# A hybrid SSD, attention and MoE block: DVE's order in the attention, and the order of weight loads in the engines' loop

## The chip, the cores and the metric

The kernel runs on one core of a Trainium2 chip. The metric is the device time of one execution in microseconds (us); less is better. Input and output are float32 in DRAM.

## The reference

One layer on 512 tokens of width 1024: an SSD branch and a sliding-window attention branch side by side, merged, and behind them a mixture of 64 small experts with six experts for each token. Two parts of it matter here:

```python
# attention, in chunks of 64 queries against a band of 128 keys
scores = einsum("bckld,bcskd->...", qc, kb) * d ** -0.5 - slopes * dist
m = maximum(max(scores), sink)
pexp = exp(scores - m)
probs = pexp / (sum(pexp) + exp(sink - m))
out = einsum(probs, vb)
# experts
for e in range(64):
    hid = silu(n @ e_gate[e]) * (n @ e_up[e])
    out = out + (hid @ e_down[e]) * combine[:, e:e + 1]
```

## The kernel before

Every engine (PE, DVE, ACT, POOL and SP, which issues most DMAs) has an instruction stream of its own, written out by hand, and waits for the others by counting semaphores. What stands behind a wait on an engine waits too.

**The attention** goes over eight chunks of queries (`NCH`). For chunk c, PE does in this order: four of the eight steps of a product of the other branch (`ssd_branch`, L1702), the transposes of the chunk's softmax weights (`turn_weights`, L1680), the other four steps of `ssd_branch`, the product with the values (`values`, L1692) and the scores of chunk c+2 (`qk`, L1666). On DVE `scores(c)` adds the position bias to the scores in PSUM, reduces them to their maximum and ends with its negative (L1121 to L1127); ACT takes eight exponentials with their sums from that (`exponentials(c)`, L865), and `weights(c)` on DVE divides by the sum (L1132 to L1134), in the tile `prob`, a view of `seg` with one half for even and one for odd chunks. PE's transposes of chunk c wait for `prob_done`, the end of `weights(c)`. ACT's order for a chunk is: the exponentials of chunk c+1, the copy of chunk c's transposed weights out of PSUM (L877), for which `values(c)` waits by `pT_done`, and two more copies. Between chunks DVE also does two `late_step`s (L1143, L1146), each a multiply-add over a 512 KB load that POOL asks for, four ahead; 16 of the 32 stand behind the last chunk.

In DVE's loop `scores(c + 1)` stands ahead of `weights(c)`.

**The experts.** Rows of tokens are gathered for a unit of work, multiplied with gate and up weights (`gate_up`, L1862), and the hidden rows with the down weights (`down`, L1870). A unit is one expert with up to 128 rows or a pair of experts with up to 64 rows each; there are 42. The first 36 are written out (units 0 to 35). The last six are pairs, which all engines do in a loop (`Fori`) over a table of experts that is made from the routing; with these inputs the loop's body, six pairs, runs once. They are called pairs 36 to 41 here. PE's order in a unit n is: `gate_up(n)`, the transposes of the next unit's rows (L1850), `down(n-1)`, the transposes of unit n's hidden rows (L1877).

The weights lie in six slots, so three pairs' worth. One expert's gate, up and down weights are three loads of 1 MB each, all of them in SP's one queue. SP refills a slot's gate and up halves when PE's `gate_up` of its former user is done (semaphore `gu_ready`) and its down half when that unit's `down` is done (`ey_ready`). In the written-out part SP asks in iteration n for the gates and ups behind `gate_up(n)`, and then for the downs that go with the gates of iteration n-1, behind `down(n-1)`. In the loop it asked so:

```python
sp.wait_ge(gu_ready, j * LAST + (BEFORE - SLOTS // 2 + m + 1))
for i in range(2):
    load_gu(slots[i], ids[i])
sp.wait_ge(ey_ready, j * LAST + (BEFORE - SLOTS // 2 + m + 1))
for i in range(2):
    load_dn(slots[i], ids[i])
```

For m = 0 to 5 these are the weights of pairs 36+m; the first wait is for `gate_up(33+m)`, the second for `down(33+m)`, which PE does behind `gate_up(34+m)`.

**The end.** DVE scales each unit's rows (`rows_out`, L1360) and POOL scatters them to DRAM (L707), six rows for a token. When pair 39's scatter has landed, SP reads all rows back in twelve loads of 1 MB (`read_rows`, L527), again in its own queue; DVE and PE add them to the residual (L1438, L1465, L1969, L1974), DVE normalises, and the output is stored. The rows of pairs 40 and 41 are added from SBUF by PE.

Of the kernel before, what the change touches and what calls it, by code (L numbers as in the profile page):

```python
# [29 lines left out]
NCH = SEQ // CHUNK  # L30
# [22 lines left out]
SLOTS = 6  # L53
# [3 lines left out]
LAST = 6  # L57
SEQ0 = FIXED + 3 * PAIRED
KINDS = "FP" * FIXED + "SPSPSSP" * (PAIRED // 4)
BEFORE = len(KINDS)  # L60
# [29 lines left out]
def hybrid_ssd_swa_moe_adaln_block(nc, a):  # L90
# [51 lines left out]
    with ExitStack() as ctx:  # L142
# [3 lines left out]
        def sem(name):  # L146
            return ctx.enter_context(nc.semaphore(name))
# [77 lines left out]
        def flat(ap):  # L225
            return ap.rearrange("p a b -> p (a b)")
# [36 lines left out]
        def over(ap, n):  # L263

            return ap.unsqueeze(2).broadcast_to([ap.shape[0], ap.shape[1], n])
# [4 lines left out]
        def dn(s):  # L270
            return dn_lo[:, s - 2, :, :] if s in (2, 3) else dn_hi[:, s if s < 2 else s - 2, :, :]
# [97 lines left out]
        ht_ready, hT_done, ey_ready, ey_dve = sem("ht_ready"), sem("hidT_done"), sem("ey_ready"), sem("ey_dve")  # L369
# [38 lines left out]
        def _(sp):  # L408
# [54 lines left out]
            def which(src, e):  # L463
                return src[e] if isinstance(e, int) else src[bass.ds(e, 1)].rearrange("o p k f -> (o p) k f")

            def load_gu(s, e):
                sp.dma_start(gu(s)[:, 0, :, :], which(w_gate, e)).then_inc(gu_in[s], 16)  # L467
                sp.dma_start(gu(s)[:, 1, :, :], which(w_up, e)).then_inc(gu_in[s], 16)  # L468

            def load_dn(s, e):  # L470
                sp.dma_start(dn(s)[:, :, :], which(w_down, e)).then_inc(dn_in[s], 16)  # L471
# [8 lines left out]
            def expert(r):  # L480
                return sp.value_load(order[0:1, r:r + 1], min_val=0, max_val=NE - 1)  # L481

            ids = [expert(r) for r in FIRST]
# [8 lines left out]
            for un in range(BEFORE):  # L492
                ids = [expert(r) for r in REFILL[un]]
# [10 lines left out]
            with sp.Fori(0, count) as j:  # L504
                for m in range(LAST):
                    ids = [sp.value_load(table[0:1, bass.ds(j * (2 * LAST) + (2 * m + i), 1)], min_val=0,  # L506
                                         max_val=EMPTY) & (NE - 1) for i in range(2)]
                    slots = [SLOT[SEQ0 + 2 * m + i] for i in range(2)]
                    for i in range(2):
                        sp.to_reg(ids[i])  # L510
                    sp.wait_ge(gu_ready, j * LAST + (BEFORE - SLOTS // 2 + m + 1))
                    for i in range(2):
                        load_gu(slots[i], ids[i])
                    sp.wait_ge(ey_ready, j * LAST + (BEFORE - SLOTS // 2 + m + 1))
                    for i in range(2):
                        load_dn(slots[i], ids[i])
            units, each = count * LAST + BEFORE, count * (16 * LAST // 2) + 16 * BEFORE // 2
            others, free = each - 16, [units - 2, units - 1]
            sp.to_reg(units), sp.to_reg(others), sp.to_reg(free[0]), sp.to_reg(free[1])
# [448 lines left out]
        def _(dve):  # L968
            steps = [0]

            def chain(ins):

                steps[0] += 1
                ins.then_inc(dve_step, 1)
                dve.wait_ge(dve_step, steps[0])
# [138 lines left out]
            def scores(c):  # L1114
                s0 = CHUNK if c == 0 else 0
                dve.wait_ge(s_ready, c + 1)
                if c >= 2:
                    dve.wait_ge(pT_ready, c - 1)
                S = prob[:, c % 2, :, s0:]
                b = 2 + 2 * (c % 2)  # L1120
                dve.tensor_tensor(S, flat(ps[:, b:b + 2, :]).rearrange("p (j s) -> p j s", s=P)[:, :, s0:],  # L1121
                                  alibi[:, :, s0:], ALU.add).then_inc(s_read, 1)
                dve.wait_ge(s_read, c + 1)
                chain(dve.tensor_reduce(mx[:, c % 2, :], S, AX.X, ALU.max))
                chain(dve.tensor_tensor(mx[:, c % 2, :], mx[:, c % 2, :], sinkc[:, :], ALU.max))
                dve.tensor_tensor(dsink[:, c % 2, :], sinkc[:, :], mx[:, c % 2, :], ALU.subtract)
                dve.tensor_scalar(nmx[:, c % 2, :], mx[:, c % 2, :], -1.0, None, ALU.mult).then_inc(nmx_done, 1)  # L1127

            def weights(c):
                s0 = CHUNK if c == 0 else 0  # L1130
                dve.wait_ge(exp_done, c + 1)
                chain(dve.tensor_tensor(den[:, c % 2, :], rsum[:, c % 2, :], esink[:, c % 2, :], ALU.add))  # L1132
                chain(dve.reciprocal(den[:, c % 2, :], den[:, c % 2, :]))
                dve.tensor_tensor(prob[:, c % 2, :, s0:], prob[:, c % 2, :, s0:], over(den[:, c % 2, :], P - s0),  # L1134
                                  ALU.mult).then_inc(prob_done, 1)
# [3 lines left out]
            def late_step(m):  # L1139
                s, k = m // KC, m % KC  # L1140
                dve.wait_ge(late_in[m % 4], 16 * (m // 4 + 1))
                if k == 0:
                    dve.tensor_scalar(late_acc[:, s, :], h[:, m % 4, :], silc[:, 0:1], None, ALU.mult).then_inc(late_used, 1)  # L1143
                else:
                    dve.wait_ge(late_used, m)
                    dve.scalar_tensor_tensor(out=late_acc[:, s, :], in0=h[:, m % 4, :], scalar=silc[:, k:k + 1],  # L1146
                                             in1=late_acc[:, s, :], op0=ALU.mult, op1=ALU.add).then_inc(late_used, 1)

            scores(0)
            for c in range(NCH):  # L1150
                if c + 1 < NCH:
                    scores(c + 1)
                weights(c)
                for m in range(2 * c, 2 * c + 2):
                    late_step(m)
            for m in range(2 * NCH, NLATE):
# [861 lines left out]
```

## Time and profile before

| | us |
|---|---|
| median of 3 runs | 1268.61 |
| lowest and highest run | 1268.25, 1270.86 |
| the profiled execution, its own time | 1268.09 |
| its span in the trace | 1266.3 |
| PE busy | 1181.1 |
| DVE busy | 480.8 |
| ACT busy | 246.4 |
| POOL busy | 192.0 |

The span runs from the first to the last instruction of the trace; all times of rows count from its start. Idle time is given in square brackets ahead of an instruction, with what ended it; "issue" there is a wait of which the profile shows no releaser. "DMA share" is the busy share of the core's 16 DMA engines, over each of which every load is spread. A load's landing is counted when the last of them is done. A granted clock (PEclk) of 1.00 is 2.4 GHz, 0.50 is 1.2 GHz.

### The profile page before, as it was taken

The page shows a single profiled execution, that of the slowest core. Times are in us where ns is not written, and L with a number is a line of the kernel's source. Part 1 is how long each engine was busy: PE and PEld are TensorE (multiplying, and loading weights), DVE is VectorE, ACT ScalarE, POOL GpSimd, SP SyncE. Part 2 cuts the span into 40 slices and gives each one's busy share as a digit, 9 for nine tenths or more (in the row PEclk, how much of TensorE's full clock was granted, in tenths as well). Part 3 has the DMA queues.
Part 4 walks back from the last instruction along what each step waited for, and adds up shares of the span by engine and source line. Part 5 has one row for each costly group of instructions (what it writes and reads, how often), then busy time and mean ns, then how long its engine had stood idle before and what let it go on. Part 6 is the DMA issues. An engine that isn't in the chain of part 4 may idle for free. (4 is left out here: it accounts for less than half of the span.)

```text
span 1266.3 us, 13416 instructions
## 1 busy us (share of the span) xinstructions
PE 1181.1 (93%) x4799; PEld 606.4 (48%) x4799; DVE 480.8 (38%) x1007; ACT 246.4 (19%) x611; POOL 192.0 (15%) x320
## 2 busy tenths in 40 slices
PE   4999999998999999999999999999999998978896
PEld 2535875565554444458854434444444343423332
DVE  5677024565564411104765222322222222212257
ACT  2141122234340100001121221221212121201111
POOL 5000010201012000010261212122121112111100
PEclk9999999999999999999999999999999999988998
DMA  9732232214549932227256999999999999999966
GB/s 301 201 123 76 67 134 91 87 56 137 163 127 357 410 136 67 99 97 328 76 198 271 333 421 421 423 423 422 415 408 409 406 397 395 399 390 389 397 259 261
DMA packets 110985, 334.66 MB, mean 264 GB/s; under 512 B 14356, under 2 KB 67688, under 8 KB 83912
## 3 DMA queue, kind: packets, MB, share of 16 engines
q1 hardware_dynamic: 87824, 269.37, 55.4%
q0 software_dynamic: 18400, 47.10, 10.3%
q10 hardware_dynamic: 4696, 17.35, 3.4%
q8 instruction: 38, 0.62, 0.2%
q14 instruction: 27, 0.22, 0.0%
HBM read 314.49 MB, written 38.35 MB: 279 GB/s over the span
## 5 line engine op out<-in xcount | busy, mean ns | idle before, releaser
L1862 PE MATMUL ps<-gu_hi,xsT 128*64 128x512 f32 (+1 forms) x704 | 243.3, 614 | 26.1 <-DMA gu_hi<-in_exp_w_up_dram 10.3
L1862 PE MATMUL ps<-gu_lo,xsT 128*64 128x512 f32 (+1 forms) x320 | 149.0, 620 | 11.8 <-issue 6.3
L1862 PEld LDWEIGHTS ps<-gu_hi,xsT 128*64 128x64 f32 (+1 forms) x704 | 84.4, 155 | 134.9 <-issue 133.1
L1364 DVE SCALAR_TENSOR_TENSOR hid<-ps,wgt,gated 128x256 f32<-128x256 f32 x42 | 20.3, 484 | 306.1 <-ACT gated L942 306.1
L1870 PE MATMUL ps<-dn_hi,hidT 128*64 128x512 f32 (+1 forms) x352 | 119.9, 597 | 1.1 <-DVE hn L1360 1.1
L1509 PE MATMUL ps<-n1T,ring 128*128 128x512 f32 x256 | 111.9, 593 | 0.0
L1739 PE MATMUL ps<-n1T,ring 128*128 128x512 f32 x256 | 110.9, 592 | 0.7 <-ACT attT L882 0.7
L707 POOL DMA_INDIRECT expert_rows<-hn,meta x40 | 40.0, 1001 | 397.2 <-DVE hn L1360 352.0
L1360 DVE TENSOR_TENSOR hn<-ps,g_row 128x1024 f32<-128x1024 f32 x42 | 51.4, 1225 | 91.6 <-PE ps L1870 91.4
L1862 PEld LDWEIGHTS ps<-gu_lo,xsT 128*64 128x64 f32 (+1 forms) x320 | 51.7, 167 | 64.8 <-issue 64.7
L942 ACT ACTIVATE gated<-ps 128x256 f32<-128x256 f32 x42 | 16.1, 384 | 332.4 <-PE ps L1862 332.4
L1739 PEld LDWEIGHTS ps<-n1T,ring 128*128 128x128 f32 x256 | 48.6, 190 | 61.6 <-issue 60.7
L1509 PEld LDWEIGHTS ps<-n1T,ring 128*128 128x128 f32 x256 | 48.1, 190 | 58.7 <-issue 58.7
L1870 PE MATMUL ps<-dn_lo,hidT 128*64 128x512 f32 (+1 forms) x160 | 72.5, 596 | 0.2 <-DMA dn_hi<-in_exp_w_down_dram 0.2
L1517 PE MATMUL ps<-ring,n1T 128*128 128x256 f32 x320 | 70.3, 380 | 0.0
L932 ACT ACTIVATE xsT<-ps,mod 128x128 f32<-128x128 f32 x172 | 64.8, 457 | 28.5 <-PE ps L1850 28.5
L1517 PEld LDWEIGHTS ps<-ring,n1T 128*128 128x128 f32 x320 | 60.5, 190 | 9.2 <-issue 1.2
L1870 PEld LDWEIGHTS ps<-dn_hi,hidT 128*64 128x64 f32 (+1 forms) x352 | 38.7, 150 | 48.1 <-issue 46.2
L1354 DVE TENSOR_SCALAR xsT<-ps,mod 128x128 f32<-128x128 f32 x172 | 58.8, 404 | 7.2 <-PE ps L1850 7.2
L1702 PE MATMUL ps<-xbcT,ring 128*128 128x512 f32 x128 | 58.4, 599 | 0.0
L1754 PE MATMUL ps<-ring,raw 128*128 128x256 f32 x256 | 56.6, 380 | 1.7 <-DVE work L1196 1.7
L1850 PEld LDWEIGHTS ps<-ident,hn 128*128 128x128 f32 x344 | 42.9, 191 | 31.2 <-issue 27.5
(336 smaller groups left out, 1329.6 us busy)
## 6 DMA issues: line engine op xcount, KB each, us to landing
gu_hi<-in_exp_w_gate_dram SPq DMA_DIRECT2D x44, 1024.0 KB, 18.6
gu_hi<-in_exp_w_up_dram SPq DMA_DIRECT2D x44, 1024.0 KB, 30.8
dn_hi<-in_exp_w_down_dram SPq DMA_DIRECT2D x44, 1024.0 KB, 29.1
ring<-in_w_in_dram SPq DMA_DIRECT2D x21, 1024.0 KB, 5.5
gu_lo<-in_exp_w_gate_dram SPq DMA_DIRECT2D x20, 1024.0 KB
gu_lo<-in_exp_w_up_dram SPq DMA_DIRECT2D x20, 1024.0 KB
dn_lo<-in_exp_w_down_dram SPq DMA_DIRECT2D x20, 1024.0 KB
h<-in_ada_w_dram POOLq DMA_DIRECT2D x32, 512.0 KB, 5.4
```

The costliest lines, as they stand in the source:

```text
L707: pool.indirect_dma_start(out=rows_d[:, :], out_offset=bass.IndirectOffsetOnAxis(ap=meta[:, c, 1:2], axis=0), in_=ys[:, b, :], in_offset=N ...
L932: ins = act.activation(xsT[:, b, k, :], ps[:, 0, P * k:P * k + P], ACT.Identity, bias=B2[:, k:k + 1], scale=A2[:, k:k + 1])
L1354: ins = dve.tensor_scalar(xsT[:, b, k, :], ps[:, 1, P * (k - 4):P * (k - 4) + P], A2[:, k:k + 1], B2[:, k:k + 1], ALU.mult, ALU.add)
L1360: dve.tensor_tensor(ys[:, b, :], flat(ps[:, 5:7, :]), g2_row[:, :], ALU.mult).then_inc(ey_dve, 1)
L1509: ins = pe.matmul(bank, w[:, k, lo:lo + P], n1T[:, k, :], start=(k == 0), stop=(k == KC - 1))
L1517: ins = pe.matmul(bank[:, 0:WB], n1T[:, k, P * t:P * t + P], w[:, k, :], start=(k == 0), stop=(k == KC - 1))
L1702: ins = pe.matmul(ps[:, 1, :], w[:, k, P * (m % 2):P * (m % 2) + P], uT[:, k, :], start=(k == 0), stop=(k == KC - 1))
L1739: ins = pe.matmul(ps[:, 4 * jj + b, :], w[:, k, P * jj:P * jj + P], src[:, k, :], start=(k == 0), stop=(k == KC - 1))
L1754: ins = pe.matmul(ps[:, 2 * (t % 2) + b // 2, WB * (b % 2):WB * (b % 2) + WB], mergedT[:, k, P * t:P * t + P], w[:, k, :], start=(k == 0), ...
L1850: ins = pe.transpose(ps[:, k // 4, P * (k % 4):P * (k % 4) + P], xs[:, b, :].rearrange("p (f k) -> p k f", k=KC)[:, k, :], ident[:, :])
L1862: ins = pe.matmul(ps[rows, 2 + b, :], xsT[:, b, k, rows], gu(s)[:, :, k, :], start=(k == 0), stop=(k == KC - 1))
L1870: ins = pe.matmul(ps[rows, 5 + half, :], hidT[:, jj, rows], dn(s)[:, jj, BANK * half:BANK * half + BANK], start=(jj == 0), stop=(jj == 1))
```

## The change

Two places, both in the order of work; no instruction is added or taken away on DVE, and SP issues the same loads.

In the attention DVE does `scores(0)` and `scores(1)` first, and from then on `weights(c)` ahead of `scores(c + 1)`. In SP's loop the down weights of pair 36+m are asked for behind the gates and ups of pair 37+m; those of the last pair follow behind the loop's last pair. The semaphore values that the downs wait for are the same as before.

```diff
--- before.py
+++ after.py
@@ -511,9 +511,14 @@
                     sp.wait_ge(gu_ready, j * LAST + (BEFORE - SLOTS // 2 + m + 1))
                     for i in range(2):
                         load_gu(slots[i], ids[i])
-                    sp.wait_ge(ey_ready, j * LAST + (BEFORE - SLOTS // 2 + m + 1))
-                    for i in range(2):
-                        load_dn(slots[i], ids[i])
+                    if m >= 1:
+                        sp.wait_ge(ey_ready, j * LAST + (BEFORE - SLOTS // 2 + m))
+                        for i in range(2):
+                            load_dn(before[i][0], before[i][1])
+                    before = list(zip(slots, ids))
+                sp.wait_ge(ey_ready, j * LAST + (BEFORE - SLOTS // 2 + LAST))
+                for i in range(2):
+                    load_dn(before[i][0], before[i][1])
             units, each = count * LAST + BEFORE, count * (16 * LAST // 2) + 16 * BEFORE // 2
@@ -1147,10 +1152,11 @@
             scores(0)
+            scores(1)
             for c in range(NCH):
-                if c + 1 < NCH:
+                weights(c)
+                if 1 <= c < NCH - 1:
                     scores(c + 1)
-                weights(c)
                 for m in range(2 * c, 2 * c + 2):
                     late_step(m)
```

DVE, one chunk in the middle of the attention, before (L1121 to L1127 are `scores(c + 1)`, L1132 to L1134 `weights(c)`; lines of the changed kernel are higher by five):

```order
L1121 TENSOR_TENSOR seg<-ps,alibi 128x1024 [waits pT_ready,s_ready]
L1124 TENSOR_REDUCE mx<-seg 128x8 [waits s_read]
L1125 TENSOR_TENSOR mx<-mx,sinkc 128x8 [waits dve_step]
L1126 TENSOR_TENSOR dsink<-sinkc,mx 128x8 [waits dve_step]
L1127 TENSOR_SCALAR nmx<-mx 128x8
L1132 TENSOR_TENSOR den<-rsum,esink 128x8 [waits exp_done]
L1133 RECIPROCAL den<-den 128x8 [waits dve_step]
L1134 TENSOR_TENSOR seg<-seg,den 128x1024 [waits dve_step]
L1146 SCALAR_TENSOR_TENSOR siluz<-h,small,siluz 128x1024 [waits late_used,late_in2]
L1146 SCALAR_TENSOR_TENSOR siluz<-h,small,siluz 128x1024 [waits late_used,late_in3]
```

The same chunk in the changed kernel:

```order
L1137 TENSOR_TENSOR den<-rsum,esink 128x8 [waits exp_done]
L1138 RECIPROCAL den<-den 128x8 [waits dve_step]
L1139 TENSOR_TENSOR seg<-seg,den 128x1024 [waits dve_step]
L1126 TENSOR_TENSOR seg<-ps,alibi 128x1024 [waits pT_ready,s_ready]
L1129 TENSOR_REDUCE mx<-seg 128x8 [waits s_read]
L1130 TENSOR_TENSOR mx<-mx,sinkc 128x8 [waits dve_step]
L1131 TENSOR_TENSOR dsink<-sinkc,mx 128x8 [waits dve_step]
L1132 TENSOR_SCALAR nmx<-mx 128x8
L1151 SCALAR_TENSOR_TENSOR siluz<-h,small,siluz 128x1024 [waits late_used,late_in2]
L1151 SCALAR_TENSOR_TENSOR siluz<-h,small,siluz 128x1024 [waits late_used,late_in3]
```

The three instructions that make the weights have moved from behind the wait for `s_ready` (PE's `qk`) to ahead of it.

SP, the loads of the loop's last pair and what stands behind them (`dn_lo` and `dn_hi` are the slots' down halves):

```order
 L467 DMA gu_lo<-in_exp_w_gate_dram 128x2048
 L468 DMA gu_lo<-in_exp_w_up_dram 128x2048
+L471 DMA dn_lo<-in_exp_w_down_dram 128x2048 [waits ey_ready]
+L471 DMA dn_hi<-in_exp_w_down_dram 128x2048
 L471 DMA dn_hi<-in_exp_w_down_dram 128x2048 [waits ey_ready]
 L471 DMA dn_lo<-in_exp_w_down_dram 128x2048
```

Two pairs' downs stand now at the end, one behind the other; ahead of them each pair's gates and ups have moved up by one pair's downs.

## Rows read from the trace of the kernel before

**Rows 1.** the page: busy time of PE; two lines of its 40 equal slices

```profile
PE 1181.1 (93%) x4799; PEld 606.4 (48%) x4799; DVE 480.8 (38%) x1007; ACT 246.4 (19%) x611; POOL 192.0 (15%) x320
...
PEclk9999999999999999999999999999999999988998
DMA  9732232214549932227256999999999999999966
```

**Rows 2.** timeline of PE, DVE, ACT, one chunk: start, length, line, [idle, releaser]

```profile
320.74 3.70 PE L1702 MATMUL ps<-xbcT,ring 128*128 128x512 f32 x8
325.44 1.09 PE L1680 MATMUL ps<-ident,seg 128*128 128x128 f32 x8 [1.00 <-DVE seg L1134]
...
329.90 1.15 PE L1692 MATMUL ps<-turned,v_odd 128*64 128x64 f32 x32
...
320.85 1.23 DVE L1121 TENSOR_TENSOR seg<-ps,alibi 128x1024 f32<-128x1024 f32 x1 [5.03 <-PE ps L1666]
...
323.65 0.17 DVE L1127 TENSOR_SCALAR nmx<-mx 128x8 f32<-128x8 f32 x1
...
324.16 1.23 DVE L1134 TENSOR_TENSOR seg<-seg,den 128x1024 f32<-128x1024 f32 x1
325.30 2.67 DVE L1146 SCALAR_TENSOR_TENSOR siluz<-h,small,siluz 128x1024 f32<-128x1024 f32 x2
...
323.85 0.40 ACT L865 ACTIVATE seg<-seg,nmx 128x128 f32<-128x128 f32 x1 [4.30 <-DVE nmx L1127]
...
327.04 1.00 ACT L877 ACTIVATE turned<-ps 128x1024 f32<-128x1024 f32 x1
```

**Rows 3.** the line L1134 alone: who waited for it, us, times

```profile
  PE ps L1680: 6.8, 7
```

**Rows 4.** timeline of DVE and PE behind the attention

```profile
421.37 1.28 DVE L1146 SCALAR_TENSOR_TENSOR siluz<-h,small,siluz 128x1024 f32<-128x1024 f32 x1 [1.74 <-DMA h<-in_ada_w_dram]
...
430.61 1.88 PE L1724 MATMUL ps<-siluz,ones 128*128 128x512 f32 x4
```

**Rows 5.** timeline of PE in the engines' loop, pairs 36, 39, 40, 41

```profile
1130.58 9.35 PE L1862 MATMUL ps<-gu_hi,xsT 128*64 128x512 f32 x32 [8.81 <-DMA gu_hi<-in_exp_w_up_dram]
...
1179.45 7.09 PE L1862 MATMUL ps<-gu_hi,xsT 128*64 128x512 f32 x32 [0.98 <-DMA gu_hi<-in_exp_w_up_dram]
...
1195.57 0.61 PE L1862 MATMUL ps<-gu_lo,xsT 128*64 128x512 f32 x1 [3.92 <-DMA gu_hi<-in_exp_w_up_dram]
...
1205.37 3.65 PE L1870 MATMUL ps<-dn_hi,hidT 128*64 128x512 f32 x16
...
1210.97 0.61 PE L1862 MATMUL ps<-gu_hi,xsT 128*64 128x512 f32 x1 [1.52 <-DMA gu_lo<-in_exp_w_up_dram]
```

**Rows 6.** timeline of SP's DMA queue

```profile
1182.45 2.31 SPq L468 DMA_DIRECT2D gu_lo<-in_exp_w_up_dram  x1
...
1191.68 0.38 SPq L471 DMA_DIRECT2D dn_lo<-in_exp_w_down_dram  x1
...
1216.25 0.81 SPq L527 DMA_DIRECT2D gu_hi<-expert_rows  x2
```

**Rows 7.** windows: length, PE, PEld, DVE, ACT, POOL busy, PEclk, DMA share, GB/s

```profile
1188.00:1200.00 12.00, 8.08 (x32) 2.96 (x30) 2.48 (x7) 1.56 (x5) 2.36 (x4) 0.86 1.01 423
...
1206.00:1208.00 2.00, 2.00 (x13) 0.58 (x9) 0.84 (x3) 0.98 (x3) 0.00 (x0) 1.00 0.27 115
1216.00:1216.50 0.50, 0.50 (x4) 0.17 (x2) 0.00 (x0) 0.00 (x0) 0.00 (x0) 1.00 0.00 0
1217.00:1217.50 0.50, 0.50 (x6) 0.17 (x2) 0.00 (x0) 0.00 (x0) 0.00 (x0) 1.00 1.13 213
```

**Rows 8.** timeline of POOL, the scatter of pair 39's rows

```profile
1211.84 0.99 POOL L707 DMA_INDIRECT expert_rows<-hn,meta  x1 [15.15 <-issue]
```

**Rows 9.** the chain that ended last, and DVE's timeline there

```profile
1223.14 22.43 DMA gu_hi<-expert_rows
...
1245.59 5.04 DVE L1438 TENSOR_TENSOR h<-h,gu_hi 128x1024 f32<-128x1024 f32 x4 [1.08 <-DMA gu_hi<-expert_rows]
```

## The prediction

> **What bounds the kernel now.** I read the page first. PE is busy for 1181.1 us of a span of 1266.3, and the DMA engines are full for its last third [rows 1]. So time can be won where PE waits, or, late in the kernel, where the DMA engines do. The timeline of the attention comes next, since one half of the change is there. PE's stream is one piece but for one gap a chunk: it ends its four steps of `ssd_branch` at 324.44, and its transposes start at 325.44, after 1.00 us of waiting for L1134, the end of `weights` [rows 2]. The line's own view puts 6.8 us on seven such waits [rows 3]. Then the engines' loop: PE starts pair 36 at 1130.58 and pair 41 at 1210.97, both as their last gate or up load lands [rows 5]. Five pairs take 80.4 us, 16.1 each, while PE's own work on a pair is 1195.57 less the wait of 3.92 and less 1179.45, so 12.2, of which 7.09 are the gates and ups and 3.65 the downs [rows 5]. There the loads set the pace. Last the end of the loop, by the windows of the DMA engines and the chain: the read-back of the rows, and behind it DVE's adds [rows 6 to 9].
>
> **Part 1, the attention.** Before, `weights(c)` stands behind `scores(c + 1)`, which waits for PE's `qk`, so it can't start before PE is at `ssd_branch(c)`: scores 320.85 to 323.82, weights until 325.39, and PE needs them at 324.44 [rows 2]. What `weights` needs itself is the chunk's exponentials. Those of chunk c+1 are done at 327.04, where ACT goes on to its copy [rows 2], 6.3 us behind the start of `ssd_branch(c)`. In the new order DVE has its two late steps behind the scores: 323.82 + 2.67 = 326.5. So the next weights run from 327.1 to 327.1 + 1.66 = 328.8 (1.66 is 325.39 less 323.73), and PE wants them not before about 335.6, when the next four steps are over. The wait goes, with some 6 us of cover.
>
> What could be late next is ACT's copy of the transposed weights, which stands behind the exponentials of the next chunk. The scores still start as `qk` ends, since the weights are out of the way by then, so the copy still ends at 328.04. PE needs it 1.00 earlier than before, at 328.90 [rows 2]. 0.86 us are left, and no new wait comes. How many chunks: seven waits of 6.8 us, six of them of 1.00 (chunks 1 to 6), which is 6.0, and 0.8 for chunk 0, whose order of `scores(1)` and `weights(0)` stays. Chunk 7 has no scores ahead of its weights. **Gain 6.0 us.** It is PE's time, and what follows hangs on PE. The late steps end at 421.37 + 1.28 = 422.65 and are wanted at 430.61 [rows 4]: if they did not move up at all, PE would want them at 424.6 and still find them. The bounds of this part are 0 (ACT's copy or another thing takes the gap) and 6.8 (all of it goes).
>
> **Part 2, the loads.** Every load is spread over 16 DMA engines. Until 1200 all are busy (share 1.01), but at 1206 to 1208 the share is 0.27, while PE still waits until 1210.6 for pair 41's last load, asked for at 1182.45 [rows 5, 6, 7]. So a few engines lag some 10 us behind the others, and a load has landed when these are done with it. They set the loop's pace. The time of 1 MB on them is at most 16.1/6 = 2.7 us.
>
> Ahead of the gates and ups of pair 37+m now stand 2 MB less, the downs of pair 36+m. So those of pairs 37 to 41 land 2 x 2.7 = 5.4 us earlier on the lagging engines; they are asked for early enough, since SP no longer waits for a `down` ahead of them, and they are in the queue for about 28 us (1182.45 to 1210.6). The downs come 2 MB behind the next pair's gates, 5.4 us, and PE needs them about 8.1 us after these (12.2 less 3.65 and an estimated 0.4 for the short transposes behind). They are not waited for. So PE does pair 41 about 5.4 us earlier, at 1205.6 in before's times.
>
> But the end is set by what comes behind. After pair 41's gates and ups, the last downs are owed: 2 MB before, so until about 1216 on the lagging engines, and the windows agree: the share is 0.00 at 1216.0 to 1216.5 and 1.13 at 1217.0 to 1217.5, when the read-back starts [rows 7], issued at 1216.25 [rows 6]. The sum of all bytes ahead of the read-back is unchanged. So however early PE is, the lagging engines start it at 1215.5 to 1216 and not at 1217. The issue itself waits for pair 39's scatter: started 1211.84 [rows 8], behind `down(39)`, which runs 1205.37 to 1209.0 [rows 5]; 5.4 us earlier gives 1206.4, and the issue about 1211. That is early enough. The lagging engines gain their idle time of 1.0 to 1.5 us, and something of the ramp behind it. I take 2.0. DVE has at present a wait of 1.08 for the tenth load of the read-back (landing at 1223.14 + 22.43 = 1245.57) and has no other wait that matters from there to the last normalisation [rows 9]. DVE and PE would be there 5 us earlier, so that landing sets the end, and it comes 2.0 earlier. **Gain 2.0 us**; bounds 0 and 5.4. I am near the lower end since the rows of the windows show how little idle time there is to be had.
>
> By the Trainium skill ("DMA: Bandwidth & Descriptors", section "Queues, rings and completion order") each of the 16 engines consumes its own ring of a queue in order. By that rule a reorder within the queue moves landings but not the time at which the lagging engines are through, which is the 2.0; without it, by PE's gain alone, the part would be 5.4. The windows agree with the rule where 0.27 of the engines are busy and a landing is still out.
>
> **The sum** is made against the profiled execution: 1268.09 - 6.0 - 2.0 = 1260.1. It is 0.5 below the median of the runs, so the median to expect is 1260.6, and I say 1260.5.
>
> **The rivals.**
>
> A. *The attention alone gains*: 1262.6. In the new order PE's waits for loads are spread otherwise: none before pair 37, about 1 us before 38, about 4 us before 39 and 40 and 3 before 41. Before, a wait of 8.81 was followed by gates and ups of 9.35 instead of 7.09 us, at a clock of 1.2 GHz for a while [rows 5]. If that follows each of three waits, pairs 39 to 41 are later by 2 to 3 us each, partly absorbed by the waits themselves, and the scatter of pair 39 comes late enough to start the read-back at 1216 again. For it: the windows give a clock of 0.86 behind a wait of only 3.92 [rows 5, 7]. Against it: the margin is 5 us. Chance 0.2. The Trainium skill ("TensorE: Matmul & The Clock Gate", "HAM oscillation") states that waits for loads which recur can bring the clock down each time; that is the rule that speaks against this half, and here it would cost what is said above.
>
> B. *The loads gain in full*: 1268.6 - 6.0 - 5.4 = 1257.2. The lagging engines are not the same ones all the time, or the read-back, started at 1211 on the others, relieves them. For it: ten loads of the read-back take 28.6 us (1217.0 to 1245.57), 2.9 each, against 2.5 at the 423 GB/s of a full window [rows 7, 9], so there is something to relieve. Against it: the 0.00 window. Chance 0.15.
>
> C. *The attention's gap moves to another wait*: PE waits for ACT's copy before `values` instead of for the weights. It decides if the scores start more than 0.86 late. If DVE's weights were still in the way (1.66 late), PE would wait 0.8, six times: 4.8 of the 6.0 are lost, 1265.4. Chance 0.08.
>
> D. *Slower than before*: the downs, now behind the next pair's gates and ups, are what PE waits for. It decides when 2 MB need more than 8.1 us on the lagging engines instead of 5.4. Slower by more than 8 + 2.6 us in sum takes over 2.1 us on each of five pairs, 10.2 us for 2 MB. With 11 us the time would be 1268.6 - 6.0 + 5 x 2.9 = 1277.1. Rows 5 speak against it: no interval of pairs shows such a pace. Chance 0.02.
>
> E. *It does not do what it says*: the lagging engines' idle time and PE's gap return elsewhere, and the time stays at 1268.6. Chance 0.03.
>
> **How the numbers follow.** The forecast has 0.52, A 0.2, B 0.15, C 0.08, E 0.03, D 0.02. The range takes in A (1262.6) and B (1257.2) with half a microsecond to a whole one for the runs, 1256.6 to 1263.6. About 0.2% or 2.5 us is what a measurement of this kernel can tell from no change. A, B, C and the forecast are faster by more: 0.95 of the chance, of which I take 0.02 for shapes of C in which less is left. Faster 0.93, same 0.05, slower 0.02.
>
> **What the changed profile would show.** Right: L1680 (now another line number) has no wait for DVE in chunks 1 to 6, chunks come every 11.1 us instead of 12.1, ACT's copy ends ahead of PE's `values`. Pair 41's gates start some 11 us earlier in absolute time than 1210.97 (6.0 and 5.4), the read-back's DMA starts some 8 earlier than 1217.0, with no window at 0.00 between, and DVE waits 3 to 5 us for read-back loads instead of 1.08. Wrong: a wait of PE before L1692, or for down weights at L1870; a read-back that starts 6 us earlier only (A) or 11 us earlier on all engines (B).

## The result, and the profile after

The change takes 1257.9 us (median of 4 runs, 1256.99 to 1258.93), the kernel before beside it 1269.36 (4 runs, 1268.25 to 1270.86): the ratio is 0.9915, interval 0.9903 to 0.9927. A second measurement of the change gave 1257.67 and 0.9912 (0.9896 to 0.9929). I said 1260.5, with a range of 1256.6 to 1263.6: the sign and the range hold, and the time is some 2.6 us below the forecast.

The profiled execution took 1258.93 us, the slowest of the four; its span is 1257.2; PE is busy for as long as before [rows 1], and the DMA engines are full for the same third. From the page of the changed kernel:

```profile
PE 1181.8 (94%) x4799; PEld 607.9 (48%) x4799; DVE 481.3 (38%) x1007; ACT 246.1 (20%) x611; POOL 191.6 (15%) x320
...
DMA  9732242224559942237256999999999999999966
```

**The attention.** The timeline of the changed kernel, the same chunk as in [rows 2] (PE, DVE, ACT; start, length, line, then idle time and its releaser in brackets where there was one):

```profile
320.40 3.70 PE L1708 MATMUL ps<-xbcT,ring 128*128 128x512 f32 x8
...
323.94 1.04 PE L1686 MATMUL ps<-ident,seg 128*128 128x128 f32 x8
...
324.81 3.60 PE L1708 MATMUL ps<-xbcT,ring 128*128 128x512 f32 x8
...
328.34 1.15 PE L1698 MATMUL ps<-turned,v_odd 128*64 128x64 f32 x32
...
320.52 1.23 DVE L1126 TENSOR_TENSOR seg<-ps,alibi 128x1024 f32<-128x1024 f32 x1 [2.92 <-PE ps L1672]
...
323.39 2.67 DVE L1151 SCALAR_TENSOR_TENSOR siluz<-h,small,siluz 128x1024 f32<-128x1024 f32 x2
326.83 0.17 DVE L1137 TENSOR_TENSOR den<-rsum,esink 128x8 f32<-128x8 f32 x1 [0.78 <-ACT esink L872]
...
327.27 1.22 DVE L1139 TENSOR_TENSOR seg<-seg,den 128x1024 f32<-128x1024 f32 x1
...
323.51 0.40 ACT L870 ACTIVATE seg<-seg,nmx 128x128 f32<-128x128 f32 x1 [4.29 <-DVE nmx L1132]
...
326.71 1.00 ACT L882 ACTIVATE turned<-ps 128x1024 f32<-128x1024 f32 x1
```

PE goes from `ssd_branch` (L1708) to the transposes (L1686) with no wait. The weights (L1137 to L1139) run from 326.83 to 328.49, right behind ACT's exponentials; the prediction said 327.1 to 328.8. ACT's copy ends at 327.71 and PE's `values` (L1698) start at 328.34, 0.63 us later. A chunk takes 328.34 less 317.42, 10.92 us, where it took 329.90 less 317.76, 12.14, before. The line that makes the weights, alone (who waited for it: us, times), answers to [rows 3]; what is left is chunk 0:

```profile
  PE ps L1686: 0.8, 1
```

**The engines' loop.** PE's timeline at the gates of pairs 36, 38, 39, 40 and 41 (pair 37 starts at 1138.40 without a wait), which answers to [rows 5]:

```profile
1123.70 9.66 PE L1868 MATMUL ps<-gu_hi,xsT 128*64 128x512 f32 x32 [8.23 <-DMA gu_hi<-in_exp_w_up_dram]
...
1150.99 0.61 PE L1868 MATMUL ps<-gu_hi,xsT 128*64 128x512 f32 x1 [0.40 <-DMA gu_lo<-in_exp_w_up_dram]
...
1167.12 1.94 PE L1868 MATMUL ps<-gu_hi,xsT 128*64 128x512 f32 x3 [3.93 <-DMA gu_hi<-in_exp_w_up_dram]
...
1183.20 0.77 PE L1868 MATMUL ps<-gu_lo,xsT 128*64 128x512 f32 x1 [2.54 <-DMA gu_hi<-in_exp_w_up_dram]
...
1198.67 0.61 PE L1868 MATMUL ps<-gu_hi,xsT 128*64 128x512 f32 x1 [1.58 <-DMA gu_lo<-in_exp_w_up_dram]
```

There is no wait for down weights. To compare the loops I count from the start of the merge behind the attention, 389.31 before and 382.87 after, so that the attention's gain is left out. So counted, pair 41 starts at 821.7 before and 815.8 after, 5.9 us earlier (5.4 were forecast). Windows of the changed kernel (length; busy time of PE, PEld, DVE, ACT, POOL; PEclk, DMA share, GB/s): the gates and ups of pairs 38, 39 and 40, then the end of the drain and the start of the read-back, which answers to [rows 7]:

```profile
1150.99:1158.08 7.09, 7.09 (x33) 2.69 (x33) 0.73 (x3) 0.02 (x1) 2.36 (x4) 1.00 1.01 423
1167.12:1175.56 8.44, 8.44 (x33) 2.87 (x33) 0.00 (x0) 0.00 (x0) 1.00 (x1) 0.84 1.01 410
1183.20:1191.98 8.78, 8.78 (x33) 3.17 (x33) 0.00 (x0) 0.00 (x0) 1.61 (x4) 0.81 0.85 353
...
1204.00:1206.00 2.00, 2.00 (x12) 0.68 (x8) 0.00 (x0) 0.21 (x1) 0.00 (x0) 1.00 0.13 53
1206.00:1208.00 2.00, 2.00 (x14) 1.13 (x14) 1.60 (x5) 1.30 (x5) 0.00 (x0) 1.00 0.07 29
1207.50:1208.00 0.50, 0.50 (x4) 0.14 (x2) 0.50 (x3) 0.50 (x3) 0.00 (x0) 1.00 0.04 16
1208.00:1208.50 0.50, 0.50 (x4) 0.14 (x2) 0.25 (x1) 0.38 (x2) 0.00 (x0) 1.00 1.53 229
```

Pair 38, behind a wait of 0.40, has the full clock and its 7.09 us; pairs 39 and 40, behind waits of 3.93 and 2.54, have 0.84 and 0.81 and take 8.44 and 8.78. The engines' share falls below 0.15 at 1204, and of 16 engines 0.07 is one: the last one or two are still busy when the read-back begins.

**The read-back.** Of the changed kernel, POOL's timeline (the scatter of pair 39), SP's queue, the chain that ended last (start, length, what), and DVE's timeline, which answer to [rows 8, 6, 9]:

```profile
1199.47 0.99 POOL L712 DMA_INDIRECT expert_rows<-hn,meta  x1 [13.78 <-issue]
...
1180.69 1.55 SPq L471 DMA_DIRECT2D dn_lo<-in_exp_w_down_dram  x1
1207.27 0.81 SPq L532 DMA_DIRECT2D gu_hi<-expert_rows  x2
...
1199.47 7.75 DMA expert_rows<-hn,meta
1207.24 0.03 issue
1207.27 0.34 SPq L532
...
1212.43 23.98 DMA gu_hi<-expert_rows
...
1220.22 5.00 DVE L1444 TENSOR_TENSOR h<-h,gu_hi 128x1024 f32<-128x1024 f32 x4 [0.69 <-DMA gu_hi<-expert_rows]
...
1229.04 5.00 DVE L1444 TENSOR_TENSOR h<-h,gu_lo 128x1024 f32<-128x1024 f32 x4 [2.57 <-DMA gu_lo<-expert_rows]
...
1236.43 5.05 DVE L1444 TENSOR_TENSOR h<-h,gu_hi 128x1024 f32<-128x1024 f32 x4 [1.07 <-DMA gu_hi<-expert_rows]
```

Before, the scatter started at 1211.84 [rows 8] and the read-back was issued at 1216.25 [rows 6], 4.4 us later. Now the scatter starts at 1199.47, and 7.75 us pass until it lands and releases the issue. Counted from the merge, the scatter starts 5.9 earlier, the issue 2.5 earlier (824.4, before 826.9), and DVE's wait for the tenth load ends 2.7 earlier (853.6, before 856.3). So the scatter's earlier start of 5.9, less the 3.4 by which its landing took longer (7.8 instead of 4.4), is the 2.5. DVE waits 0.69, 2.57 and 1.07 us for loads, 4.3 in all (3 to 5 forecast).

### The profile page after: what moved, and what is told of

The parts are those of the page before. It is cut to its first block and busy times, and to the rows that moved or that the text cites. A ratio compares the mean times of both kernels' runs of the same rounds, so it can differ in the third digit from the quotient of the medians.

```text
span 1257.2 us, 13416 instructions
## 1 busy us (share of the span) xinstructions
PE 1181.8 (94%) x4799; PEld 607.9 (48%) x4799; DVE 481.3 (38%) x1007; ACT 246.1 (20%) x611; POOL 191.6 (15%) x320
## 2 busy tenths in 40 slices
DMA packets 110985, 334.66 MB, mean 266 GB/s; under 512 B 14356, under 2 KB 67688, under 8 KB 83912
## 5 line engine op out<-in xcount | busy, mean ns | idle before, releaser
L947 ACT ACTIVATE gated<-ps 128x256 f32<-128x256 f32 x42 | 16.1, 383 | 327.1 <-PE ps L1868 327.1
L1708 PE MATMUL ps<-xbcT,ring 128*128 128x512 f32 x128 | 58.4, 599 | 0.0
```

Source lines behind the costliest of these rows:

```text
L1708: ins = pe.matmul(ps[:, 1, :], w[:, k, P * (m % 2):P * (m % 2) + P], uT[:, k, :], start=(k == 0), stop=(k == KC - 1))
```

## The experiments

Nine kernels, each timed beside the kernel before. First the two halves of the change, each alone.

### The attention alone

Kernel before, with the change's order in DVE only:

```diff
             scores(0)
+            scores(1)
             for c in range(NCH):
-                if c + 1 < NCH:
+                weights(c)
+                if 1 <= c < NCH - 1:
                     scores(c + 1)
-                weights(c)
```

Expected:

> The kernel before with the new order of the attention alone; the loop asks for its downs as before. In the profile of the change the attention is 7.3 us shorter than before (first scores to the merge: 87.9 against 95.3), not 6.0. If nothing behind it gives that back, this kernel is 7.3 us faster than before. Rival: the stages behind are bound by transfers that do not move up, and the gain is 6 us or less. Second rival: the attention is worth more than its PE time, 9 us or more, since it also moves the loads.

Measured: 1261.44 us (5 runs, 1260.63 to 1262.4), before 1268.75; ratio 0.9943 (0.9929 to 0.9956), so 7.3 us less. From the first scores to the merge the attention took 389.31 less 294.05, 95.3 us, before, and 382.87 less 294.94, 87.9, in the changed kernel: 7.3 too. This half is worth 7.3 us and not the 6.0 of my sum. Behind the merge (383.24) the end comes as it did: the read-back is issued at 1209.77, 826.5 from the merge, before 826.9.

### The loads alone

Kernel before, with the downs one pair later in SP's loop, DVE as before. The edit is the first piece of the change's diff.

> The kernel before with the new order of loads in the loop alone. Theory of the lagging DMA engines: PE starts pair 41's gates 5 to 6 us earlier than before (1210.97), the read-back 2 to 3 us earlier than 1217.0, and the time falls by 2 to 3 us. Rival (all of PE's lead counts): 5.4 us or more. Rival (all is lost at the read-back): within 1 us of before.

Measured: 1265.3 us (10 runs, 1263.87 to 1267.01), ratio 0.9971 (0.9962 to 0.9981): 3.5 us less, interval 2.4 to 4.8. The halves add up: 7.3 and 3.5 are 10.8, and the whole change has 0.9912 to 0.9915 of 1268.75, 10.8 to 11.2. Its scatter starts at 1207.29 and its read-back is issued at 1214.78, 7.5 us later, as in the changed kernel; from the merge (390.46) the issue is at 824.3. This was not the full 5.4 of rival B, and half a microsecond more than the 2 to 3 expected.

### The changed kernel again

The changed kernel, word for word, as a second measurement beside the runs that leave work out below.

> The changed kernel itself once more, so that it stands beside the others of this call and has more runs: 10 to 11.5 us under before, the sum of its two halves measured alone (7.3 and 3.5).

Measured: 1257.67 us (4 runs, 1255.56 to 1259.0). The issue of the read-back is at 1207.22, the waits at the gates 8.59, 3.94, 2.20 and 1.55 us. From the merge (383.31) the scatter starts at 816.4 and the issue comes at 823.9.

### Scores 1.2 us later

What is next in the attention, and how near? In the changed kernel one more addition over 1024 columns stands between the wait for `qk` and the scores, in chunks 2 to 7:

```diff
                     dve.wait_ge(pT_ready, c - 1)
+                    dve.tensor_tensor(work[:, 4 * SEQ:4 * SEQ + D], flat(alibi[:, :, :]), flat(alibi[:, :, :]), ALU.add)
```

> The change with one more add of 1024 columns on DVE (1.2 us, its result unused) between the wait for a chunk's scores and the scores themselves, in chunks 2 to 7. In the changed kernel ACT's copy of the turned weights ends 0.63 us ahead of PE's values. If ACT's copy is next in line, PE waits about 0.6 us a chunk before the values, 3.6 us in all against the change. If there is more cover than that (the copy is not what comes next), the time stays within 1 us of the change.

Measured: 1261.11 us (5 runs), ratio 0.9938 (0.9924 to 0.9952), 3.2 to 3.4 above the two measurements of the change. PE's waits in the attention, by the waits view of that kernel (waiter <- releaser: us in total, times, longest), and its timeline in one chunk:

```profile
PE ps L1699 <- ACT turned L882: 2.9, 6, 0.5
...
328.86 1.00 ACT L882 ACTIVATE turned<-ps 128x1024 f32<-128x1024 f32 x1
...
329.92 0.50 PE L1699 MATMUL ps<-turned,v_odd 128*64 128x64 f32 x9 [0.49 <-ACT turned L882]
```

So the copy (L882) is what comes next, as rival C had it. Some 1.2 us of delay met a slack of 0.63 and left 0.6; the rows show 0.49 for each of six chunks, 2.9 in all, and 3.2 to 3.4 were measured, which the intervals of the ratios do not tell apart.

This kernel's loop is word for word the change's, and its profiled execution differs there mainly in one thing: PE did the gates and ups of pair 40 at the full clock. From its windows, its queues of POOL and SP, and its windows around the issue of the read-back:

```profile
1186.87:1193.96 7.09, 7.09 (x33) 2.68 (x33) 0.00 (x0) 0.00 (x0) 1.95 (x4) 1.00 0.93 387
...
1201.44 0.99 POOL L712 DMA_INDIRECT expert_rows<-hn,meta  x1 [11.74 <-issue]
...
1209.10 0.81 SPq L532 DMA_DIRECT2D gu_hi<-expert_rows  x2
...
1209.00:1209.50 0.50, 0.50 (x6) 0.20 (x4) 0.00 (x0) 0.00 (x0) 0.00 (x0) 1.00 0.12 49
```

Counted from the merge (386.67), pair 40 starts at 800.2, in the change at 800.3. It takes 7.09 us instead of 8.78, the scatter starts at 814.8 instead of 816.6, and the read-back is issued at 822.4 instead of 824.4, while two of the 16 engines (0.12) are still busy. So what released the issue was not the end of the lagging engines' work: it came with the landing of pair 39's scatter, whose start hangs on PE, 7.7 us behind that start. In the change these are 7.8 us, in its repetition 7.5 and in the loads alone 7.5.

### Downs two pairs later

Does the wait of rival D exist, and from which point? In the changed kernel the downs of a pair are asked for behind the gates and ups of the pair after the next:

```diff
-                    if m >= 1:
-                        sp.wait_ge(ey_ready, j * LAST + (BEFORE - SLOTS // 2 + m))
-                        for i in range(2):
-                            load_dn(before[i][0], before[i][1])
-                    before = list(zip(slots, ids))
+                    if m >= 2:
+                        sp.wait_ge(ey_ready, j * LAST + (BEFORE - SLOTS // 2 + m - 1))
+                        for s, e in waiting.pop(0):
+                            load_dn(s, e)
+                    waiting.append(list(zip(slots, ids)))
```

(and two such groups behind the loop).

> The change with the loop's downs asked for two pairs later instead of one. By the queue in order, a pair's downs then land about 16 us behind the next pair's gates and PE, which wants them 8.1 us behind these, waits for them at every pair from 36 on. The loads still set the pace, but the down of pair 39 and its scatter come some 8 us later than in the change, so the read-back starts 2 to 4 us later and the time is 2 to 4 us over the change. Rival (order in the queue does not matter, since the DMA engines are full anyway): the same time as the change, and no wait of PE for downs.

Measured: 1261.12 us (5 runs), ratio 0.9935 (0.9922 to 0.9949), 3.2 to 3.4 above the change. PE's timeline of that kernel at its waits in the loop:

```profile
1152.09 5.49 PE L1878 MATMUL ps<-dn_hi,hidT 128*64 128x512 f32 x16 [5.12 <-DMA dn_hi<-in_exp_w_down_dram]
...
1167.71 0.61 PE L1878 MATMUL ps<-dn_lo,hidT 128*64 128x512 f32 x1 [1.59 <-DMA dn_hi<-in_exp_w_down_dram]
...
1184.26 1.08 PE L1878 MATMUL ps<-dn_hi,hidT 128*64 128x512 f32 x1 [4.35 <-DMA dn_lo<-in_exp_w_down_dram]
...
1200.28 3.65 PE L1878 MATMUL ps<-dn_hi,hidT 128*64 128x512 f32 x16 [1.01 <-DMA dn_hi<-in_exp_w_down_dram]
```

Now PE waits at the downs (L1878), 12.1 us in all, and no longer at the gates of pairs 38 to 41. The mechanism of rival D is real and begins one pair further on. Its price is small against 12.1, since a wait at the downs takes the place of one at the next gates, but it is all that the loads' half had gained: the scatter of pair 39 stands behind such downs, and the read-back is issued at 826.9 from the merge (383.80), where it was before.

### Without the scatters

What makes a few DMA engines lag? This is the changed kernel with the scatters' bound at row 0, so that the units' output rows are not written to DRAM (that part of the computation is left out; the instructions and their descriptors stay):

```diff
-            last_token, last_row = pool.to_reg(SEQ - 1), pool.to_reg(NROW - 1)
+            last_token, first_row = pool.to_reg(SEQ - 1), pool.to_reg(0)
...
-                    in_=ys[:, b, :], in_offset=None, bounds_check=last_row, oob_is_err=False).then_inc(scattered[b], 16)
+                    in_=ys[:, b, :], in_offset=None, bounds_check=first_row, oob_is_err=False).then_inc(scattered[b], 16)
```

> The change with all scatters of the experts' rows bounded to row 0, so that next to nothing is written (left out: the rows of units 0 to 39 in DRAM, which stay zero); the scatter instructions, their waits and semaphores stay. Theory 1: the engines that lag do so because of the scatters, which fall unevenly on the 16. Then the share falls from 1 to 0 within 2 or 3 us at the end of the expert loads instead of some 17, the gates of pair 41 start 8 us earlier or more against those of the change, and the time falls by about as much. Theory 2: the lag comes from elsewhere (gathers, or engines slow by themselves): the ramp of the share stays over 10 us long, and the time falls by 1 to 4 us, for the bytes that are not written.

Measured: 1219.1 us (4 runs, 1217.5 to 1219.42), ratio 0.9614 (0.9598 to 0.9631), 38.6 below the changed kernel beside it. The windows of that kernel at the end of its loads (columns as above), and PE's timeline at the gates of pair 41:

```profile
1158.00:1160.00 2.00, 1.33 (x7) 0.60 (x9) 0.00 (x0) 0.00 (x0) 1.32 (x3) 1.00 0.99 418
1160.00:1162.00 2.00, 2.00 (x12) 0.84 (x10) 0.00 (x0) 0.00 (x0) 1.04 (x1) 1.00 0.87 361
1162.00:1164.00 2.00, 2.00 (x12) 0.85 (x10) 0.00 (x0) 0.00 (x0) 0.00 (x0) 1.00 0.47 177
1164.00:1166.00 2.00, 2.00 (x11) 0.68 (x8) 0.00 (x0) 0.21 (x1) 0.00 (x0) 1.00 0.27 111
...
1158.66 0.61 PE L1868 MATMUL ps<-gu_hi,xsT 128*64 128x512 f32 x1 [2.68 <-DMA gu_lo<-in_exp_w_up_dram]
```

Pair 41's last load lands some 0.3 us ahead of its gates, at 1158.3, while all engines are still busy; in the changed kernel it landed at 1198.3, some 9 us after the share had begun to fall. So most of the unequal load of the engines comes with the scatters, as I supposed, but not all is shown to: the share falls from full to 0.27 in some 5 us and stands there when the read-back is issued at 1165.47, so that the rest of the drain can't be seen. The bytes cost more than the lag: 12.4 MB less are moved (322.29 instead of 334.66 by the pages), which is 29 us at the 423 GB/s of a full window [rows 7], and that makes three quarters of the 38.6. I had expected a gain of 8 us or more, about as much as the lag, and had left the bytes out. The remaining 9 us go by the name of lag here without a run that shows it.

### Without the last pair's downs

Is it the backlog on the lagging engines that starts the read-back? In the changed kernel the downs behind the loop, 2 MB, are left out, and pair 41 uses the weights of pair 38 that lie in these slots:

```diff
-                sp.wait_ge(ey_ready, j * LAST + (BEFORE - SLOTS // 2 + LAST))
-                for i in range(2):
-                    load_dn(before[i][0], before[i][1])
```

> The change without the loads of the last pair's down weights, 2 MB (left out: pair 41 is computed with the downs of pair 38, which lie in its slots). If the read-back is held up by the lagging engines' backlog, that ends 4.9 us earlier here, the scatter of pair 39 lands 3 to 4 us after its start instead of 7.8, the read-back starts 4 to 5 us earlier than in the change, and the time falls by 4 to 5 us. If PE's chain to the scatter is what holds it and the scatter takes 7.8 us anyway, the read-back starts at the same time and the gain is under 1 us.

Measured: 1254.57 us (4 runs), ratio 0.9893 (0.9876 to 0.991), 3.1 below the changed kernel beside it. Its scatter starts at 1198.76. From its timeline, the issue of the read-back on SP's queue, and DVE's adds behind it:

```profile
1204.90 0.81 SPq L529 DMA_DIRECT2D gu_hi<-expert_rows  x2
...
1219.71 7.51 DVE L1441 TENSOR_TENSOR h<-h,gu_hi 128x1024 f32<-128x1024 f32 x6
...
1234.62 5.00 DVE L1441 TENSOR_TENSOR h<-h,gu_hi 128x1024 f32<-128x1024 f32 x4
```

DVE has no wait for a load left. Counted from the merge (384.01) the issue is at 820.9 instead of 824.4, but not all of these 3.5 us belong to the loads: here too pair 40 had the full clock, and the scatter started at 814.8 instead of 816.6. The execution of "Scores 1.2 us later" has that start and all loads; against it the scatter landed in 6.1 instead of 7.7 us, and the issue came 1.5 earlier. So bytes behind which a scatter stands do lengthen its landing, by some 1.5 us for these 2 MB, but neither expectation came out: it was to land in 3 to 4 us by the first and in 7.8 by the second. From there on DVE's adds are the bound, one behind the other, so that shorter waits for the read-back's loads alone would give nothing more.

### Neighbouring entries 8 partitions apart

Can the lag be cured? A unit's filled rows lie at the low partitions of each half of 64, and I supposed that neighbouring partitions go by the same DMA engine. In the changed kernel the upper and the lower three bits of an entry's place in its 64 change sides:

```diff
+                dve.tensor_scalar(up, at, 3, 0xE00, ALU.logical_shift_left, ALU.bitwise_and)
+                dve.tensor_scalar(down, at, 3, 0x1C0, ALU.logical_shift_right, ALU.bitwise_and)
+                chain(dve.tensor_scalar(at, at, 0x1F03F, None, ALU.bitwise_and))
+                chain(dve.tensor_tensor(up, up, down, ALU.bitwise_or))
+                dve.tensor_tensor(at, at, up, ALU.bitwise_or).then_inc(ordered, 1)
```

(`at` is the place of the entry, 64 to a block, by 64, plus the expert.)

> The changed kernel, with the place of an entry in its list of 64 rewritten as it is chosen: of the six bits of the place the upper three and the lower three change sides, so that neighbouring entries come to stand 8 partitions apart instead of side by side (five small DVE instructions more per tile of tokens, two of them on the path before the lists are read, together under 1 us). The gathers and scatters of a unit still move as many rows, but these are spread over all partitions. Theory 1 (the engines lag because a unit's filled rows lie in the low partitions of either half, and so on the same DMA engines unit after unit, while all sixteen share the weights evenly): the fall of the DMA share ahead of the read-back, which took from about 1190 to 1207 us, shrinks to a few us; the area under it (share 0.3 to 0.5 over some 17 us) is 8 to 10 us that all engines together do not need, so pair 41 is gated 3 to 8 us earlier and the read-back's loads are issued 4 to 9 us earlier, until DVE and PE bound the end: 1249 to 1254 us. Rival (the engines lag for another reason, such as packets of a scatter that take long on any engine): the ramp stays as it is and the time is that of the changed kernel or up to 1 us above it, 1257.5 to 1258.7 us.

Measured: 1270.02 us (11 runs, 1269.18 to 1271.64), ratio 1.0015 (1.0006 to 1.0024): 12 to 13 us above the change, all of its gain gone. The loop begins 0.9 us later; the rest is lost while loads stream, as the windows of this kernel and of the changed one show (40 us each, the second pair of rows is the changed kernel's):

```profile
1060.00:1100.00 40.00, 36.99 (x133) 15.88 (x132) 8.40 (x21) 6.44 (x17) 6.39 (x12) 0.91 0.96 367
1100.00:1140.00 40.00, 30.03 (x108) 12.69 (x108) 8.03 (x19) 4.94 (x13) 7.67 (x13) 0.87 0.98 379
```

```profile
1060.00:1100.00 40.00, 37.13 (x146) 17.26 (x145) 10.25 (x25) 7.19 (x19) 7.09 (x12) 1.00 1.00 397
1100.00:1140.00 40.00, 31.77 (x127) 12.41 (x127) 9.47 (x24) 6.42 (x17) 5.31 (x9) 0.87 1.00 400
```

Packets and bytes are the same (110985, 334.66 MB), but 367 and 379 GB/s are moved where the change has 397 and 400, and the share has fallen to 0.96 and 0.98. Engines without work account for about half of the lower rate (4 and 2% of 8 and 5%); for the other half they were busy and moved less, which no run explains. Its drain is no shorter and comes later; the read-back is issued at 1219.69. So where the filled rows lie does matter, and this placement makes it worse, where I had assumed the opposite.

### Places mixed by expert

From that I formed another theory, that row p goes by engine p modulo 16, and had the lower four bits of a place mixed with the expert's number:

```diff
+                dve.tensor_scalar(low, low, 6, 0x3C0, ALU.logical_shift_left, ALU.bitwise_and)
...
+                dve.tensor_tensor(at, at, low, ALU.bitwise_xor).then_inc(ordered, 1)
```

> The changed kernel, with the lower four bits of an entry's place in its list combined (exclusive or) with the lower four bits of its expert's number, by two small DVE instructions more per tile of tokens. The same rows are moved from the same half; which residues of the partition by 16 the filled ones take now differs by expert. With neighbouring entries 8 partitions apart the time was 12 us above the change at the same packets and bytes, so placement matters, but not as assumed. Theory 1 (row p of a gather or scatter goes by DMA engine p modulo 16): by the counts of this input's lists the most loaded engine had 217 of the 3072 rows, mean 192; with entries 8 apart 307, here 196. At 4 KB a row in each direction and 423 GB/s over 16 engines (26.4 GB/s each) an excess of 25 rows is 7.8 us of one engine, of 115 rows 36 us, of 4 rows 1.2 us. The most loaded engine sets when a unit's weights are complete, so up to 6.6 us of lag go: the drain ahead of the read-back is 3 to 6 us shorter, the time 1252 to 1255.5 us. Rival (8 neighbouring partitions by one engine, as assumed before): mixing the lower four bits keeps each group of 16 on two engines, nothing changes: 1257 to 1258.5 us. Second rival (the order of addresses in DRAM matters, since neighbouring entries of a list no longer follow each other): no gain, or a loss.

Measured: 1258.12 us (5 runs, 1257.5 to 1259.08), ratio 0.992 (0.9906 to 0.9933): the same as the change. Its share falls from 0.94 at 1188 to 1190 to 0.17 at 1204 to 1206, nearly the ramp of the change. This theory falls too: it wanted 3 to 6 us. With neither assumed map can both runs be explained. Others, such as one by blocks of four neighbouring partitions, were not tried, nor was the second rival, the order of addresses in DRAM, told apart from them; which engine serves which row stays open. No version here beats the change.

## Why the prediction was right, and where it was off

- **Part 1, the attention: the mechanism was right, its size 1.3 us too small** (6.0 in the sum, 7.3 by the run of this half alone). The step that failed is "six of them of 1.00, which is 6.0". A bracketed wait of PE counts from the modelled end of the matmuls ahead of it, 320.74 + 3.70 = 324.44 [rows 2]. Where PE doesn't wait, the next group starts before that end: in the change at 323.94, when the group ahead ends at 324.10, and it is 1.04 long instead of 1.09. 1.00 + 0.16 + 0.05 is 1.21 a chunk, the 1.22 that the two periods show. Six of them are 7.3. The kernel before shows it too, at chunk 7, where PE has no wait: the transposes start at 383.06, when the group ahead (379.52 + 3.70) ends at 383.22. My bound of 6.8, all the waits of the line's own view, was no bound for that reason.
- The cover was right. Weights ran at the forecast times, the copy's slack was 0.63 (forecast 0.86), and a delay of 1.2 us brought out exactly this wait, six times. So rival C was the next thing in line, but did not happen.
- **Part 2, the loads: right in sign, too small, and for a reason that did not hold** (2.0 in the sum; 3.5 by the run of this half, 2.4 to 4.8; 2.7 between the profiled executions). PE came 5.9 us earlier to pair 41 (5.4 forecast) and gained only half of it at the end, as forecast. The step that failed is "So however early PE is, the lagging engines start it at 1215.5 to 1216 and not at 1217". The read-back was issued at 824.4 from the merge, which in before's times is 1213.7, and its DMA followed at about 1214.4; and it was the scatter of pair 39, which hangs on PE's `down(39)`, that released it, not the end of the lagging engines' work, as the execution with pair 40 at the full clock shows (scatter 1.8 earlier, issue 2.0 earlier, two engines still busy).
- The other half of the same step is "5.4 us earlier gives 1206.4, and the issue about 1211. That is early enough": it took the 4.4 us from the scatter's start to the issue as they were before, but a scatter that starts while engines are busy takes longer to land. The starts at 822.5 to 823.4 from the merge (before, the attention alone, downs two pairs later) have the issue 3.1 to 4.4 us behind them, at 826.5 to 826.9; the five at 814.3 to 816.8 (the change, its repetition, the loads alone, scores later, places by expert) have it 7.5 to 7.8 us behind. So 5.9 less 3.4 is what the order gave in the profiled executions. That 2.0 was near 2.5 is luck: the term was the idle time of the lagging engines, and it was not this that was gained. Why the runs give 3.5 and the profiled executions 2.7 isn't shown; the change's profiled execution is the slowest of its four, with a mean clock of 0.983 against 0.985 to 0.987.
- The time of 1 MB on the lagging engines, "at most 16.1/6 = 2.7 us", held as the value for landings. Pair 41 was 5.9 us earlier from the merge, but pair 36, which the order can't touch, was 0.4 earlier as well (741.3 and 740.8); the rest is 5.4, in the loads alone 5.5 and in the repetition 5.6, for the 5.4 forecast. It isn't the time by which 2 MB less shorten the end (1.5 in the run without the last downs).
- The rule of the Trainium skill ("DMA: Bandwidth & Descriptors", "Queues, rings and completion order"), that each engine consumes its ring of a queue in order, gave the 2.0, against 5.4 without it. The landings agree with it: 5.4 to 5.6 us earlier for 2 MB less in front, and with the downs two pairs later it was these that PE waited for. The 3.5 measured lies between the two. The rule is about one queue; the scatters come by another, and my use of it left them out.
- **Rival A** (1262.6) named something that happened: the clock of pairs 39 and 40 fell to 0.84 and 0.81 behind waits of 3.93 and 2.54, at a cost of 1.4 and 1.7 us each. Pair 39's cost went into the next wait for loads. Pair 40's did not: it delayed the scatter of pair 39, and where the clock held, the read-back was issued 2.0 us earlier and the span from the merge was 1.5 us shorter (872.8, in the change 874.3). So my "margin of 5 us" against A was not there, and A cost part of the gain without taking all of it. The rule of the Trainium skill on it ("TensorE: Matmul & The Clock Gate", "HAM oscillation"), that recurring waits for loads can bring the clock down each time, agrees with these rows.
- **Rival B** (1257.2) is the nearest number to the result, for another reason: each half gave more than its term, but the loads not 5.4. **Rival D** was one pair away: it takes downs two pairs later, and even then costs 3.2 to 3.4 us against the change, so the loads' half and no more, and not 19, because my price added up waits of which each takes the place of one at the next gates. **E** fell.
- The signs to watch for came out as said but for sizes: the chunk at 10.9 and not 11.1 us, pair 41 12.3 earlier in absolute time and not 11, the read-back's load engines starting 9 earlier and not 8, without a window at 0.00 (0.04 from 1207.5 to 1208).

## What to carry to other kernels

The wait that a timeline shows ahead of a pipelined matmul understates what its removal gives, here by a fifth (1.00 shown, 1.21 gained); compare with a place where the same two groups follow each other without a wait. When a scatter's landing sets an event, count its time by what else the DMA engines have to do when it starts: here it was 3.1 to 4.4 us near the end of the drain and 7.5 to 7.8 before it, so that an earlier start gave less than half of itself. A wait moved from gates to downs costs only by what hangs on the downs, here the scatter: 3.2 to 3.4 us for 12.1 us of waits.

## What the runs showed of the hardware that I had not expected

- The scatters of output rows, 12.4 MB of 334.7, cost 38.6 us when they share the DMA engines with the weights, 29 of it at the full rate of 423 GB/s. With them the share of the DMA engines takes 17 to 19 us to fall from full to nearly nothing, and pair 41's last load lands some 9 us into that; without them it lands before the fall begins.
- The same rows at other partitions, with equal packets and bytes, cost 12 us (1270.02 against 1257.7 to 1257.9), and a milder rearrangement nothing. Two maps from rows to engines were tried as an explanation and neither fits both runs.
- The scatter of pair 39 landed 3.1 to 4.4 us after its start near the end of the drain and 7.5 to 7.8 in the middle of it. It is hardly a matter of its own bytes: in the run whose scatters write nothing it took 7.1, started with all engines full.
- A clock of 0.81 over one pair's gates and ups, 1.7 us of PE, showed up as 1.8 us at the scatter behind it and 2.0 us at the read-back.
